# A transformer pair on one core: the first conditions in blocks of 256 + 256 columns, and two products begun behind four of them

## The reference, cut to what matters

```
mod   = silu(c) @ w_mod + b_mod          # six pieces of 2048 columns: sa, ca, ga, sm, cm, gm
mod_c = silu(c_ctx) @ w_mod + b_mod
h   = rmsnorm(x, norm_attn_w)   * (1 + ca)   + sa        # 256 rows
h_c = rmsnorm(ctx, norm_attn_w) * (1 + ca_c) + sa_c      # 256 rows
p   = h @ w_in                           # columns q, k, v, u are used in this stage
p_c = h_c @ w_in                         # columns k and v
```

## Time and profile before

| | before |
|---|---|
| median of 3 runs | 2280.54 us (2280.31 to 2280.58) |
| the profiled execution | 2280.14 us, span of its instructions 2278.3 us |
| PE busy | 2244.0 us, 98% |
| DVE busy, ACT busy | 1606.3 us, 1055.9 us |
| first product on PE | 36.38 us after the start of the span |

### The profile page before, as it was taken

The page is one execution under the profiler, slowest core; times in us unless marked ns, Lnnn a source line. Parts: engine busy times, 40 slices in busy tenths (PEclk is TensorE's granted clock), DMA queues, the critical chain, the costliest instruction groups (busy, mean ns, idle before and its releaser), DMA issues.

```text
span 2278.3 us, 29999 instructions
## 1 busy us (share of the span) xinstructions
PE 2244.0 (98%) x11659; PEld 1833.5 (80%) x11659; DVE 1606.3 (71%) x2366; ACT 1055.9 (46%) x1575; POOL 72.9 (3%) x91
## 2 busy tenths in 40 slices
PE   6999999999999999999999999999999999999998
PEld 3777787877888788888888888888887888888876
DVE  3577798777888777677666565764787545589965
ACT  4443234555543644344444343454555454466644
POOL 1000001110000100000000000000000000000000
PEclk8999999999999999999999999999999999999999
DMA  9999884444689677766756555555434576432243
GB/s 373 338 314 316 298 306 153 148 147 149 222 305 322 211 266 236 236 239 225 254 191 191 189 190 181 182 185 185 162 118 151 183 234 208 159 119 93 93 143 116
DMA packets 280065, 474.56 MB, mean 208 GB/s; under 512 B 7784, under 2 KB 100288, under 8 KB 278928
## 3 DMA queue, kind: packets, MB, share of 16 engines
q1 hardware_dynamic: 276336, 460.35, 60.0%
q0 software_dynamic: 3296, 12.53, 1.6%
q10 hardware_dynamic: 320, 0.13, 0.0%
HBM read 470.89 MB, written 2.10 MB: 208 GB/s over the span
## 4 chain that ended last, share of the span: by engine, by line
PE 94%; DVE 3%; DMA 1%; issue 1%; ACT 0%; ACTq 0%; POOLq 0%; POOL 0%; DVEq 0%
PE acc L1970 63%; PE acc L1986 13%; PE acc L1990 7%; PE aux L2475 1%; PE turn L2455 1%; PE acc L2441 1%; PE aux L2019 1%; DVE arena L1750 1%; PE turn L2205 1%; DMA raw<-in_w_mod 1%; DVE wlo L1117 1%; PE turn L2067 1%; PE acc L2220 1%; PE turn L2372 0%; PE acc L2190 0%
## 5 line engine op out<-in xcount | busy, mean ns | idle before, releaser
L1117 DVE TENSOR_TENSOR wlo<-raw,whi 128x1024 fp32r<-128x1024 f32 x674 | 820.3, 1224 | 493.5 <-ACT whi L611 488.6
L611 ACT ACTIVATE whi<-raw 128x1024 fp32r<-128x1024 f32 x674 | 711.4, 1059 | 955.0 <-PE acc L1970 699.0
L1970 PE MATMUL acc<-whi,x 128*128 128x512 f32 x2176 | 551.7, 395 | 4.9 <-ACT x L693 2.7
L1970 PEld LDWEIGHTS acc<-whi,x 128*128 128x128 f32 x2176 | 403.0, 188 | 114.1 <-issue 24.8
L1986 PE MATMUL acc<-x,whi 128*128 128x512 f32 x1408 | 357.1, 395 | 0.7 <-issue 0.7
L1970 PE MATMUL acc<-wlo,x 128*128 128x512 f32 x1088 | 292.0, 390 | 0.0
L1986 PEld LDWEIGHTS acc<-x,whi 128*128 128x128 f32 x1408 | 253.4, 189 | 47.9 <-issue 1.4
L1970 PEld LDWEIGHTS acc<-wlo,x 128*128 128x128 f32 x1088 | 204.2, 188 | 43.4
L1990 PEld LDWEIGHTS acc<-x,wlo 128*128 128x128 f32 x1408 | 192.0, 190 | 14.0
L1990 PE MATMUL acc<-x,wlo 128*128 128x256 f32 x1408 | 196.1, 282 | 0.0
L1970 PE MATMUL acc<-whi,hhi 128*128 128x512 f32 x512 | 137.6, 390 | 0.0
(11 more groups left out here) (330 smaller groups left out, 2030.1 us busy)
## 6 DMA issues: line engine op xcount, KB each, us to landing
raw<-in_w_ff SPq DMA_DIRECT2D x128, 1024.0 KB, 5.5
raw<-in_w_mod SPq DMA_DIRECT2D x96, 1024.0 KB, 7.3
raw<-in_w_in SPq DMA_DIRECT2D x64, 1024.0 KB, 5.5
raw<-in_b_w_in SPq DMA_DIRECT2D x45, 1024.0 KB, 5.1
raw<-in_a_w_in SPq DMA_DIRECT2D x36, 1024.0 KB, 4.9
raw<-in_w_o SPq DMA_DIRECT2D x16, 1024.0 KB, 6.8
raw<-in_a_w_out SPq DMA_DIRECT2D x16, 1024.0 KB, 4.9
raw<-in_b_w_out SPq DMA_DIRECT2D x16, 1024.0 KB, 5.0
```

What stands on the lines that cost most here:

```text
L611: act.activation(whi[:, k % 2, on], raw[:, n % 4, on], ACT.Copy).then_inc(hi_ready, 1)
L1117: dve.tensor_tensor(wlo[:, k % 2, on], raw[:, LOAD_OF_UNIT[k] % 4, on], whi[:, k % 2, on].bitcast(F32), ALU.subtract)\
L1970: mm = pe.matmul(acc[:, bank0 + t, :], x[:, tile(kt), t * P:(t + 1) * P], w[:, u % 2, kk], start=kt == k_first and x is hi and w is whi, s ...
```

## The change

1. The eight conditions of the first quarter are cut differently. The first four loads cover 256 shift and 256 scale columns (both for the first two feature tiles, all 2048 rows), the second four the next 256 and 256. Each load is issued as two DMAs of 128x4x256, so its pieces in memory are 1 KB long where they were 2 KB. After the first four loads both scale and shift of the feature tiles 0 and 1 are known.
2. `CONDITIONS_FIRST` is 4: SP issues four conditions (`x` behind the first of them), u0 (in two halves), u1, then the other four conditions, u2, `ctx`, u3. In before u0 and u1 came behind all eight.
3. PE makes the first half (feature tiles 0 and 1) of the products u0 and u1 behind the first four conditions, then the other four conditions, then the second halves. 8, 5 and 22 transposes of the identity matrix into a free bank (`stay_busy`) are put among this.
4. Scale and shift of a pair of tiles are made apart from each other; ACT rounds x straight from PSUM (new L710) while DVE makes the unrounded value (new L1224).
5. Of the two squares of `ctx` DVE makes one (new L1365, a multiply with an accumulated sum over 128x2048), and DVE normalizes `ctx` ahead of splitting u3, not behind it. The transposes of `ctx` stand between the two halves of u3.
6. At the end of the first quarter ACT and DVE build the next left operand ahead of splitting the unit after next.

PE, from its first condition to u3, before: lines L2019 are conditions, L2034 columns, L2054 transposes of x, L1970 products.

The diff, cut to what is spoken of (waits of the DMA halves and the renamed counts are left out):

```diff
-CONDITIONS_FIRST = 8
+CONDITIONS_FIRST = 4
...
+LOADED_BEHIND[1] += (CONDITIONS1 - CONDITIONS_FIRST) * ["mod"]
...
+            if kind == "plain" and count["plain"] == 1:
+                for k, signal in ((0, first_half_in), (2, raw_in[n % 4])):
+                    sp.dma_start(raw[:, n % 4, k:k + 2], src.rearrange("(k p) n -> p k n", p=P)[:, k:k + 2]).then_inc(signal, 16)
+                return
...
+            if kind == "mod" and count["mod"] <= CONDITIONS1:
+                for h, signal in ((0, half_in[n % 4]), (1, raw_in[n % 4])):
+                    sp.dma_start(raw[:, n % 4, :, h * L:(h + 1) * L], src[:, :, h, :]).then_inc(signal, 16)
+                return
...
+            if b < 2:
+                both = a["w_mod"].rearrange("(k p) (h n) -> p k h n", p=P, n=D)
+                load("mod", both[:, 4 * k:4 * k + 4, 0:2, b * L:(b + 1) * L])
+                return
...
-            if c == 3:
+            if c == 0:
...
         def round_scaled(n):
 
-            act.wait_ge(x_scaled, n + 1)
-            act.activation(xhi[:, 2 * n:2 * n + 2, :], v3(mtmp[:, n, :], L), ACT.Copy).then_inc(hi_rounded, 1)
+            act.wait_ge(turned, n + 1)
+            act.wait_ge(cond_ready, n + 1)
+            for k in range(2):
+                kt = 2 * n + k
+                if k:
+                    act.wait_ge(x_scaled, 2 * n + 1)
+                act.activation(xhi[:, kt, :], turn[:, k, n * L:(n + 1) * L], ACT.Identity, scale=scale_x[:, kt:kt + 1],
+                               bias=shift_x[:, kt:kt + 1]).then_inc((x_rounded, hi_rounded)[k], 1)
...
-        copy_front_condition(1)
+        copy_front_condition(0)
         split_halves(0, 1)
         round_scaled(0)
+        split_halves(1, 3)
+        copy_front_condition(1)
         round_scaled(1)
-        split_halves(1, 3)
...
                 if (quarter, b) == (0, 2):
-                    take_product(products[0] + 1)
                     for n in range(2):
                         front_build(2 + n)
+                    take_product(products[0] + 1)
                     copy_front_condition(2)
-                split(u + 2, 1)
+                if (quarter, b) == (0, 1):
+                    take_product(products[0])
+                    act.wait_ge(ctx_in, 16)
+                    first_squares(T)
+                early = (quarter, b) == (0, 7)
+                if not early:
+                    split(u + 2, 1)
                 if quarter < 3 and b == LAST_COLUMNS_AT[quarter]:
                     for n in range(2):
                         front_build(4 * (quarter + 1) + n)
-                if quarter == 0:
+                if early:
+                    split(u + 2, 1)
+                if quarter == 0 and b != 1:
                     take_product(products[-1])
-                if (quarter, b) == (0, 1):
-                    act.wait_ge(ctx_in, 16)
-                    for i in range(T, 2 * T):
-                        first_squares(i)
                 if quarter and b == 1:
                     for n in range(2):
                         front_build(4 * quarter + 2 + n)
...
                 part = arena[:, i * D:(i + 1) * D]
                 dve.tensor_scalar(part, part, rstd[:, i:i + 1], None, ALU.mult).then_inc(normed, 1)
 
...
         def scale_rows(n):
 
             dve.wait_ge(turned, n + 1)
-            for k in range(2 * n, 2 * n + 2):
-                ins = dve.tensor_scalar(mtmp[:, n, (k % 2) * L:(k % 2 + 1) * L], turn[:, n, (k % 2) * L:(k % 2 + 1) * L],
-                                        scale_x[:, k:k + 1], shift_x[:, k:k + 1], ALU.mult, ALU.add)
-            ins.then_inc(x_scaled, 1)
+            dve.wait_ge(cond_ready, n + 1)
+            for k in (1, 0):
+                kt = 2 * n + k
+                if k == 0:
+                    dve.wait_ge(x_rounded, n + 1)
+                dve.tensor_scalar(mtmp[:, n, k * L:(k + 1) * L], turn[:, k, n * L:(n + 1) * L], scale_x[:, kt:kt + 1],
+                                  shift_x[:, kt:kt + 1], ALU.mult, ALU.add).then_inc(x_scaled, 1)
...
+        first_mean(0)
+        first_norm(0)
         take_front_condition(0)
+        scale_rows(0)
+        front_build(0)
+        split_halves(0, 4)
         take_front_condition(1)
-        dve.wait_ge(cond_ready, 1)
-        scale_rows(0)
         scale_rows(1)
-        front_build(0)
-        split_halves(0, 1)
         front_build(1)
-        scales(0, 1)
-        split_halves(1, 3)
         for quarter in range(4):
             for b in range(8):
                 products = [12 * quarter + p for p, (c, _) in enumerate(FRONT_PRODUCTS[quarter]) if c == b]
                 sums = FRONT_SUMS[quarter][b]
                 if quarter < 3 and b == COLUMNS_AT + 1:
                     take_front_condition(2 * (quarter + 1))
-                if (quarter, b) == (0, 2):
+                if (quarter, b) == (0, 1):
+                    dve.wait_ge(ctx_in, 16)
+                    dve.tensor_tensor_reduce(out=qkv[:, 6144:8192], in0=rows[:, D:2 * D], in1=rows[:, D:2 * D], scale=1.0, scalar=0.0,
+                                             op0=ALU.mult, op1=ALU.add, accum_out=lam[:, 7:8]).then_inc(sumsq_ready, 1)
                     first_mean(T)
                     first_norm(T)
-                norm_summed = sum_for_norm(min(sums, 1))
                 if (quarter, b) == (0, 2):
                     for n in range(2):
                         front_build(2 + n)
+                norm_summed = sum_for_norm(min(sums, 1))
                 if quarter and len(products) == 2:
                     add_product(products[0])
                 if quarter < 3 and b == LAST_COLUMNS_AT[quarter]:
...
                     finish_slab(None)
                     dve.wait_ge(norm_columns, 8)
                     dve.tensor_copy(modcol[:, :], aux[:, 1, 448:512]).then_inc(norm_taken, 1)
+                early = (quarter, b) == (0, 7)
+                if early:
+                    for n in range(2):
+                        front_build(4 + n)
                 norm_summed = sum_for_norm(max(sums - 1, 0))
                 split(8 * quarter + b + 2, 1)
                 if quarter:
...
                 if quarter and b == 1:
                     for n in range(2):
                         front_build(4 * quarter + 2 + n)
-                if quarter < 3 and b == LAST_COLUMNS_AT[quarter]:
+                if quarter < 3 and b == LAST_COLUMNS_AT[quarter] and not early:
                     for n in range(2):
                         front_build(4 * (quarter + 1) + n)
                 if quarter == 0 and b == 7:
...
         def condition(c, k, bank):
 
             n = LOAD_OF_COND[c]
...
-        for c in range(4):
-            front_condition(c)
+        front_condition(0)
+        front_condition(1)
         pe.wait_ge(first_params_in, 16 * SMALL_FIRST)
         pe.wait_ge(b_mod_in, 16)
         pe.transpose(turn[:, 0, 0:96], vec1[0:96, :], ident[0:96, 0:96])
         pe.transpose(turn[:, 0, P:P + V_END], vec2[0:V_END, :], ident[0:V_END, 0:V_END])
         pe.matmul(turn[:, 1, 0:416], sel[0:1, 0:P], param_row, start=True, stop=True).then_inc(setup_turned, 1)
-        pe.wait_ge(strips_ready, 1)
-        front_columns(0)
-        for c in range(4):
-            front_condition(4 + c)
+
+        def stay_busy(count):
+
+            for _ in range(count):
+                pe.transpose(acc[:, 3, 0:P], ident[:, :], ident[:, :])
+
+        front_condition(2)
         pe.wait_ge(normed, T)
         pe.wait_ge(cols_ready, 2)
         front_rows(0)
         front_rows(1)
+        stay_busy(8)
+        front_condition(3)
+        stay_busy(5)
+        pe.wait_ge(strips_ready, 1)
+        front_columns(0)
+        stay_busy(22)
+        for p in range(2):
+            multiply(p, 0, 1, 2 * p, 0, tiles=(0, 1), rounded=1)
+        for c in range(4):
+            front_condition(4 + c)
         front_columns(1)
         next_condition, columns = 8, 2
         for p, (quarter, (b, rows)) in enumerate((q, x) for q in range(4) for x in FRONT_PRODUCTS[q]):
             shared, u = FRONT[b][0] in "kv", 8 * quarter + b
             if p >= 2:
                 pe.wait_ge(acc_freed, p - 1)
-            for part in range(2):
+            for part in range(int(p < 2), 2):
                 hi, lo, k_first = (chi, clo, 0) if rows else (xhi, xlo, 4 * quarter)
                 mm = multiply(u, 0, 1, 2 * (p % 2), k_first, hi, lo, tiles=(2 * part, 2 * part + 1), used=rows == shared,
                               rounded=4 * quarter + 2 * rows + part + 1)
+                if (p, part) == (3, 0):
+                    pe.wait_ge(normed, 2 * T)
+                    for n in range(2):
+                        front_rows(2 + n)
             if shared and rows == 0:
                 mm.then_inc(shared_done, 1)
-            if (b, rows) == ((1, 0) if quarter else (3, 0)):
-                if quarter == 0:
-                    pe.wait_ge(normed, 2 * T)
+            if quarter and (b, rows) == (1, 0):
```

(1 more changed line is left out.)

59 lines of the change are left out of this document (36 added, 23 removed).

## The result

| | before | after |
|---|---|---|
| median | 2280.34 us (2280.02 to 2280.58, 6 runs) | 2292.43 us (2291.87 to 2294.56, 6 runs) |
| ratio | | 1.0054, 95% interval 1.0045 to 1.0064 |
| profiled execution, span | 2280.14, 2278.3 us | 2291.91, 2290.1 us |
| PE busy | 2244.0 us | 2253.4 us |

The changed kernel is 12.1 us slower (0.54%). The forecast was 2282.1 us in a range of 2278.7 to 2284.6; the result lies outside it, by 7.8 us. The prediction was wrong.

A forecast was written before the change was run, and what follows sets the result against it. The start was taken as bound by the order and number of bytes ahead of the last condition, plus a chain. Start +1.90, norm +0.6, quarter's end -0.96 made +1.54 on 2280.54: 2282.1 us, range 2278.7 to 2284.6.

The forecast's parts named there:

- first halves 26.5: Start: four conditions landed by 21.3 us plus 5.2 of chain put the first halves of u0 and u1 at 26.5.
- The split of u1 at 31.9: Start: DVE's split of u1 ends at 31.9, the eighth condition lands by 37.4, 1.2 us ahead of need.
- rival 3: Start: late first chain, split of u1 holds the eighth condition, DMA runs empty; +1 to +2 us, 2283.6; chance 10%.
- Last condition at 38.58: Start: 31.20 plus 5.42 for u0 and u1 loaded ahead plus 1.96 for 1 KB pieces gives 38.58 us.
- rival 1: Start: 1 KB pieces cost nothing, +1.90 becomes -0.06, total 2280.1 us; chance 12%.
- The same loss is likely: Start, second halves: the 1.41 us lost at half clock stays as before; ends 0 and about twice as much.
- Rival 4: Start, 38.6 to 50: TensorE stays long at 1.2 GHz; from 3.0 us further loss, 2285.1 or 2286; chance 8%.
- u3 at 58.00: End of the start stage: u3 begins at 58.00 us against 56.10 before, +1.9 us.
- DVE's square at 2.3 us: Square of the second ctx row: 2.3 us by slope, hidden; at 4.6 it would cost 1.0 us of slack.
- The thirteenth condition waits 0.6: Behind u3: the thirteenth condition lands at 78.7, PE wants it at 78.1; +0.6 us, ends 0 and 2.
- The end, -0.96: End of the first quarter: building the left operand earlier removes PE's wait for ACT, -0.96 us.
- faster by more cannot come: Whole change: u3 needs the same 18 MB, so with the 0.96 us the gain is at most 3.2 us.

The follow-up runs named there:

- e3: The changed kernel without its 35 filler transposes: 2290.60 us (ratio 1.0047 to the kernel before).
- e9: The changed kernel with ACT and DVE splitting u0 ahead of the first condition's columns: 2288.95 us (ratio 1.0036 to the kernel before).
- e4: The kernel before with each of its first eight conditions loaded by two DMAs of 256 columns, in 1 KB pieces: 2283.07 us (ratio 1.0013).
- e13: The kernel before with each of its first eight conditions loaded by two DMAs halved by rows, in 2 KB pieces: 2280.49 us (ratio 1.0001).
- e8: The changed kernel with eight more fillers behind each of conditions 5 to 8 and fourteen behind the second columns: 2288.47 us (ratio 1.0038).
- e5: The kernel before with part 6 of the change alone (next left operand built ahead of splitting the ninth unit): 2284.53 us (ratio 1.0018).
- e6: The kernel before with part 6 of the change, but DVE's sum ahead of the low parts: 2279.50 us (ratio 0.9995).
- e7: The changed kernel with all eight conditions ahead of u0 and u1 and both halves of each product together: 2286.48 us (ratio 1.0025).
- e1: The changed kernel with part 6 undone (ninth unit split before the next left operand is built): 2289.12 us (ratio 1.0039).

## Why the prediction was wrong, step by step

- **What bounds the start.** "The start is set by the order and number of bytes ahead of the last condition, plus that chain" failed. It takes for granted that SyncE may issue the next load when DMA has room. With u0 and u1 ahead of the last four conditions, the last two of these wait for a slot that DVE frees by a split, and the splits wait for the whole first chain.
- **"The fourth condition ... 21.3", first halves 26.5.** Failed: 24.76 and 29.71, 3.5 and 3.2 us late. Its data was not what was late. PE had a full list at half clock from 16.18 on (1.94 us for the second condition, then, as shown, 1.75, 1.94 and 1.83). From there to the end of the transposes it took 7.6 us; at the durations that the same rows have at full clock in before, and without a wait for data, it would be about 4.2 (estimate). So the low clock can be nearly all of the 3.5. Beside it the eight fillers of 1.04 us, counted as lying in a wait, stood among work; dropping them gives 0.8 back (e3). The chain behind it was sized rightly (4.95 for 5.18).
- **The split of u1 at 31.9, "1.2 us ahead of need".** Failed: 34.9, 3.0 late, and DMA ran at 246 GB/s. This was rival 3, at 10% and +1 to +2. There the mechanism was right and the size too small. The 1.2 us of slack never existed: it was worked out with the shortest landing of the stage, 5.5 us, and the eighth condition began 7.6 us behind the split in after and 7.3 in e9. At 7.3 the split had to end by 31.3. e9, that only lets the splits go earlier, brings 3.5 us.
- **Last condition at 38.58.** It came at 42.46, 3.9 late. By the prediction's own sum a split 3.0 late leaves 1.8 beyond the slack, and the other 2.1 are the landing (7.6 for 5.5); how much of that is the dearer pieces the trace doesn't tell. Their price was taken as 1.96 us and is 2.6 at the last condition and 2.9 in the time (e4); 0.245 a load is 0.33. The row at 355 GB/s was the right kind of row, and rival 1 (pieces cost nothing) is refuted: e13 against e4 differ in the size of the pieces alone, by 2.6 us.
- **"The same loss is likely" (1.41 us of clock).** Too small: 4.1 us from the last condition through the second halves, by e8. The traces give the clock as a share of the full one; no run shows the prediction's levels in GHz, what they show are shares of 0.50 and 1.00 with 3.75 and 2.08 us for eight multiplications. Rival 4 had its place right (38.6 to 50) and its deciding point of 3.0 us of further loss nearly: 2.7.
- **u3 at 58.00.** 64.32. The steps above make up the 6.3 us: 3.88 to the last condition, 1.06 from it to the second halves, 1.38 from their start to u3. Behind them all went as forecast (7.39 us for 7.35).
- **DVE's square at 2.3 us.** Right: 2.29, so the slope of the earlier trace rows held and 16 times its larger row (4.6) did not. **The thirteenth condition waits 0.6.** Right: 0.55. Undoing the norm takes the wait away and brings 1.2, half of which isn't the norm's by the trace.
- **The end, -0.96.** The wait went, but "the split of the ninth unit gets later on DVE by its 1.4 us of low parts, while PE needs it a whole unit later" failed twice. The split got later by the sum of 3.11 us too, which now stands behind parts that wait for ACT. And PE was the wrong one to ask: the next user of the split is SyncE, whose load behind it was issued 1.9 us after the first product (128.54 to 126.67), where in before it was 0.4 ahead. The diff in front showed the move, and the prediction didn't follow the slot. e5 against e6: 5.0 us.
- **The forecast of the case itself.** The bound "faster by more cannot come" was not put to the test. The sum had three terms of slack (1.2 us, "a whole unit", "13 lie in waits"), each worked out from when PE needs a thing. Two of them were really about when SyncE's queue moves, and both failed to the same side.

The terms as measured: pieces 2.9 (e4), early halves 6.0 (e7), end 3.3 to 4.1 (e1, e5). They sum to 12.2 to 13.0 with a change of 12.1, and the norm's share, half a us to 1.2, is part of it as well, so the sum is about one to two us too large. Up to u3 the traces show where, as far as single traces can: pieces 2.9 (58.98 for 56.10), early halves 6.8 (64.32 for 57.54), and against them the 1.4 us that e7 gains by its shorter chain, together the 8.2 of the change. The 6.0 holds the queue (3.5), the fillers (1.8) and the clock (4.0) in one, and these three overlap too: 0.8 of e9's gain at u3 is clock.

## What to carry to other kernels

Where one queue issues loads in order into slots that another engine frees, ask of each moved step when its slot comes free, and what stands behind it on the queue; that the multiplying engine needs the result "a unit later" says nothing about it. When work is moved ahead on an engine, list all that is queued there behind it (here a sum of 3.1 us), and put what waits behind what doesn't. When a stage is split to start a part early, price the smaller pieces of its loads (here 2.9 us, e4) and the loads that then have to wait for the early part (3.5 us, e9); here these two ate more than the early part hid (5.48 us by the prediction's sum). Take the landing time for such a sum from loads in the same crowd, not the shortest of the stage (here 7.3 to 7.6 us, not 5.5).
